# Gated delta rule of all chunks at once, its output made token by token inside the state chain

## What is computed

```
def gated_delta_rule(q, k, v, log_g, beta):          # 4 heads of 128, chunks of tokens
    gc = cumsum(log_g within the chunk)
    decay = exp(where(causal, gc_i - gc_j, -inf))
    kb = k * beta
    lower = where(strict, (kb @ k^T) * decay, 0)
    sol = triangular_solve(I + lower, [v * beta, kb * exp(gc)])
    u_base, w = sol
    attn = where(causal, (q @ k^T) * decay, 0)
    q_dec, k_dec = q * exp(gc), k * exp(g_last - gc)
    for each chunk, in order:
        u = u_base - w @ S
        o = q_dec @ S + attn @ u
        S = S * exp(g_last) + k_dec^T @ u
o_gdn = rms_norm(o, o_gain) * silu(gz)               # norm over the 128 of a head
mix   = concat([o_fox, o_gdn]) @ w_out
```

## Time and profile before

| quantity | value |
|---|---|
| median of 3 runs | 4125.67 us (4125.08 to 4134.72) |
| profiled execution, its time | 4139.84 us |
| profiled execution, its span | 4138.1 us |
| mean granted TensorE clock | 0.905 of full |
| busy: TensorE matmul, VectorE, ScalarE, GpSimd | 84%, 41%, 17%, 15% of the span |
| gated rule, third phase | 421.8 to 571.1 us |
| output stage, fourth phase | 571.1 to 588 us |
| forgetting attention, fifth phase | from 588.85 us |

### The profile page before, as it was taken

One profiled execution on the slowest core, in us unless ns is written; L12 is line 12 of the kernel. 1 busy time (PEld: TensorE's weight loads), 2 busy tenths in 40 slices (PEclk: granted clock), 3 DMA queues, 4 the chain that ended last, 5 costly groups with the idle time before them and its releaser, 6 DMA issues. The chain is left out here.

```text
span 4138.1 us, 48435 instructions
## 1 busy us (share of the span) xinstructions
PE 3482.5 (84%) x16676; PEld 2455.7 (59%) x16676; DVE 1704.2 (41%) x4271; ACT 697.8 (17%) x1515; POOL 605.8 (15%) x516
## 2 busy tenths in 40 slices
PE   8998768999989477998998688888779977788886
PEld 7875646887866476787786434333357764333433
DVE  2113333111122643211124576677512336676774
ACT  1001121101001111110122122222111311222221
POOL 0000000000000000000000244444300004444442
PEclk9998557999999788999998899999999998999999
DMA  4441002443422000343332599999842328999995
GB/s 169 147 151 71 0 0 76 145 156 122 151 108 99 2 3 2 122 154 132 136 130 100 237 421 421 421 422 422 357 156 83 131 92 355 421 422 421 422 421 207
DMA packets 113651, 828.17 MB, mean 200 GB/s; under 512 B 12528, under 2 KB 14064, under 8 KB 15120
## 3 DMA queue, kind: packets, MB, share of 16 engines
q0 software_dynamic: 73728, 536.90, 31.2%
q1 hardware_dynamic: 37184, 273.59, 18.0%
q10 hardware_dynamic: 2576, 15.59, 1.0%
HBM read 824.99 MB, written 1.05 MB: 200 GB/s over the span
## 5 line engine op out<-in xcount | busy, mean ns | idle before, releaser
L2090 PE MATMUL psum_all<-expert_rows,const_sb 128*128 128x512 f32 x2048 | 988.3, 641 | 265.0 <-ACT const_sb L2036 263.4
L1881 POOL DMA_INDIRECT expert_rows<-in_peer_uv_dram,head_experts x512 | 605.6, 1183 | 3463.5 <-issue 2434.3
L2090 PEld LDWEIGHTS psum_all<-expert_rows,const_sb 128*128 128x128 f32 x2048 | 409.9, 204 | 826.2 <-issue 488.4
L1971 DVE CUSTOM_DVE_ANT_0 expert_rows<-expert_rows,xn 128x1024 f32<-128x1024 f32 x512 | 618.5, 1224 | 312.2 <-DMA expert_rows<-in_peer_uv_dram,head_experts 307.1
L261 PE MATMUL psum_all<-xn,weight_ring 128*128 128x272 f32 (+1 forms) x3200 | 732.3, 392 | 0.0
L261 PEld LDWEIGHTS psum_all<-xn,weight_ring 128*128 128x128 f32 x3200 | 613.4, 192 | 118.8
L261 PE MATMUL psum_all<-hidden,weight_ring 128*128 128x272 f32 (+1 forms) x1408 | 318.6, 389 | 0.0
L261 PEld LDWEIGHTS psum_all<-hidden,weight_ring 128*128 128x128 f32 x1408 | 267.5, 190 | 50.5
L1599 PE MATMUL psum_all<-x,weight_ring 128*128 128x256 f32 x1024 | 229.0, 382 | 0.0
L2036 ACT ACTIVATE const_sb<-cst,head_weights 128x128 f32<-128x128 f32 x512 | 163.7, 390 | 321.4 <-DVE head_weights L1977 318.3
L1599 PEld LDWEIGHTS psum_all<-x,weight_ring 128*128 128x128 f32 x1024 | 192.9, 191 | 28.6 <-issue 2.9
(11 more groups left out here) (480 smaller groups left out, 3333.2 us busy)
## 6 DMA issues: line engine op xcount, KB each, us to landing
weight_ring<-in_ffn_in_dram SPq DMA_DIRECT2D x88, 1024.0 KB, 4.8
weight_ring<-in_w_in_dram SPq DMA_DIRECT2D x48, 1024.0 KB, 5.0
weight_ring<-in_ffn_out_dram SPq DMA_DIRECT2D x32, 1408.0 KB, 6.0
weight_ring<-in_peer_q_dram SPq DMA_DIRECT2D x16, 1024.0 KB, 7.9
weight_ring<-in_hyb_in_dram SPq DMA_DIRECT2D x12, 1024.0 KB, 4.8
wv<-in_w_v_dram ACTq DMA_DIRECT2D x8, 1024.0 KB, 7.7
weight_ring<-in_br_attn_dram SPq DMA_DIRECT2D x8, 1024.0 KB, 5.9
weight_ring<-in_br_lru_dram SPq DMA_DIRECT2D x8, 1024.0 KB, 6.5
```

The source lines that it names most:

```text
L1881: pool.indirect_dma_start(out=rows[:, j, :], out_offset=None, in_=a["peer_uv"], in_offset=bass.IndirectOffsetOnAxis(ap=idx[:, n, j:j + 1], ...
L1971: dve.tensor_tensor_reduce(row, row, xt[:, n, :], 1.0, 0.0, ALU.mult, ALU.add, dots[:, n, j:j + 1]).then_inc(S.dotted, 1)
L2090: mm = pe.matmul(sums(n, half), diag[:, j, :], rows[:, j, D + half * 512:D + (half + 1) * 512], start=False, stop=last and j == TOPK - 1)
```

## The change

The third phase handles all ten blocks at once: scores of the five chunks into three banks and the last blocks of each kind into others, turns by matmul against the identity in five groups, one solve with ten blocks, then a written-out chain over the chunks. `NL` of the solver takes its place in the idle region of the weight ring. A function `beside` lets VectorE make the attention products behind the solver's masks. The output of a chunk is made with tokens on partitions (`ot`), copied out by ScalarE, its squares summed by VectorE along the free axis, root on ScalarE, scaled, turned by TensorE, and multiplied by gain and gate into `mixed`, up to three steps behind the state. The fourth phase is removed. Silu of the gate goes to the end of ScalarE's stream in the first phase. The loops become straight code.

```diff
@@ solve_dve
         for l in range(1, LEVELS):
             last = level(l)
+        if beside is not None:
+            beside()
@@ first phase, ScalarE
-                        act.wait_ge(S.silu_ready, 12)
+                        act.wait_ge(S.bank_free, 4 + NZ)
+                        act.activation(z[:, 20:24, PADC:PADC + T], z[:, 20:24, PADC:PADC + T], ACT.Silu).then_inc(S.silu_ready, 1)
+                        act.wait_ge(S.silu_ready, 13)
@@ third phase, VectorE
-                            step(dve.memset(state[:, :, :], 0.0))
...
-                            with step.loop(NC - 1, 6) as c:
-                                chunk(c, True)
-                            chunk(NC - 1, False)
+                            dve.tensor_scalar(rneg[ROW_A:64, :], cum[ROW_A:64, :], -1.0, None, ALU.mult).then_inc(S.negated, 1)
+                            dve.wait_ge(S.decay_scores, 1)
+                            dve.tensor_scalar(dmat[:, MAIN_COLS], score_main(DECAY), 0.0, None, ALU.min).then_inc(S.decays, 1)
+                            dve.tensor_scalar(dmat[:, LAST_COLS], score_last(DECAY), 0.0, None, ALU.min).then_inc(S.decays, 1)
+                            dve.wait_ge(S.d_exp, 1)
+                            dve.wait_ge(S.scores, 1)
+                            dve.scalar_tensor_tensor(out=sb_.NT[:, MAIN_COLS], in0=score_main(KEYS), scalar=-1.0, in1=dmat[:, MAIN_COLS], op0=ALU.mult, op1=ALU.mult)
+                            step(dve.scalar_tensor_tensor(out=sb_.NT[:, LAST_COLS], in0=score_last(KEYS), scalar=-1.0, in1=dmat[:, LAST_COLS], op0=ALU.mult, op1=ALU.mult))
+                            def attention():
+                                step(dve.tensor_tensor(blocks3(dmat[:, :]), blocks3(dmat[:, :]), const("incl").unsqueeze(1).to_broadcast([P, BLOCKS, C]), ALU.mult))
+                                dve.wait_ge(S.scores, 2)
+                                dve.wait_ge(S.turned_in, len(turns))
+                                dve.tensor_tensor(at[:, MAIN_COLS], score_main(QUERIES), dmat[:, MAIN_COLS], ALU.mult).then_inc(S.attn_ready, 1)
+                                dve.tensor_tensor(at[:, LAST_COLS], score_last(QUERIES), dmat[:, LAST_COLS], ALU.mult).then_inc(S.attn_ready, 1)
+                            solve_dve(dve, S, step, 0, BLOCKS, sb_, solver_banks, attention)
...
+                            for c in range(NC + 3):
+                                if 1 <= c < NC:
+                                    dve.wait_ge(S.r_product, c)
+                                    dve.tensor_tensor(R[:, :, :], vt[:, 2 * c:2 * c + 2, :], psum[2][:, 0:2 * P].rearrange("p (g n) -> p g n", g=2),
+                                                      ALU.subtract).then_inc(S.r_ready, 1)
+                                if 2 <= c < NC + 2:
+                                    sum_out(c - 2)
+                                if c >= 3:
+                                    finish(c - 3)
+                                if c < NC - 1:
+                                    dve.wait_ge(S.s_product, c + 1)
...
+                                    last.then_inc(S.state_ready, 1)
+                                    dve.wait_ge(S.state_ready, c + 1)
+                                if 2 <= c < NC + 2:
+                                    scale_out(c - 2)
@@ third phase, ScalarE
+                            for c in range(NC + 2):
+                                if c < NC:
+                                    act.wait_ge(S.u_product, c + 1)
+                                    act.activation(U[:, c % 2, :, :], psum[3][:, 0:2 * P].rearrange("p (g n) -> p g n", g=2), ACT.Copy).then_inc(S.u_ready, 1)
+                                if 1 <= c <= NC:
+                                    take_out(c - 1)
+                                if c >= 2:
+                                    root(c - 2)
@@ third phase, TensorE
+                            for c in range(NC):
+                                for h, g_, q in heads:
+                                    sel = const("sel_g64", slice(ROW_A, 64), h * C, C)
+                                    o = score_block(DECAY, 2 * c + g_)[q, :]
+                                    pe.matmul(o, sel, cum[ROW_A:64, tokens(c)], start=True, stop=False)
+                                    mm = pe.matmul(o, rneg[ROW_A:64, tokens(c)], sel, start=False, stop=True)
+                            mm.then_inc(S.decay_scores, 1)
...
+                            products(KEYS, kb)
+                            for n, (_, src, first, count, bank) in enumerate(turns):
+                                if n == 3:
+                                    pe.wait_ge(S.decays, 2)
+                                if n == 4:
+                                    products(QUERIES, gq)
+                                for b in range(count):
+                                    for h in ((first + b) % 2 * 2, (first + b) % 2 * 2 + 1):
+                                        q = slice((h % 2) * C, (h % 2) * C + C)
+                                        mm = pe.matmul(bank[q, b * P:(b + 1) * P], src[:, h, tokens((first + b) // 2)], ident, start=True, stop=True)
+                                mm.then_inc(S.turned, 1)
+                            pe.wait_ge(S.turned_in, len(turns) - 1)
+                            solve_pe(pe, S, 0, BLOCKS, sb_, solver_banks)
...
+                            for c in range(NC):
+                                before = state[:, c % 2, :, :]
+                                if c:
+                                    pe.wait_ge(S.state_ready, c)
+                                    for h, g_, q in heads:
+                                        mm = pe.matmul(psum[2][q, g_ * P:(g_ + 1) * P], kbg[:, h, tokens(c)], before[:, h, :], start=True, stop=True)
+                                    mm.then_inc(S.r_product, 1)
+                                    if c >= 2:
+                                        pe.wait_ge(S.o_read, c - 1)
+                                    for h, g_, q in heads:
+                                        pe.matmul(out_block(c, g_, q), qd[:, h, tokens(c)], before[:, h, :], start=g_ == 0, stop=False)
+                                if c >= 3:
+                                    turn_out(c - 3)
...
+                                if c:
+                                    inside(c - 1)
+                                pe.wait_ge(S.u_ready, c + 1)
...
+                            inside(NC - 1)
+                            for c in range(NC - 3, NC):
+                                turn_out(c)
@@ fourth phase (silu, squares, head sums, root, reciprocal, spreading, gain, gate): removed
```

More of the change, by code:

```diff
@@ L674, in hybrid @@
-                    heads = [(h, h // 2, slice((h % 2) * C, (h % 2) * C + C)) for h in range(GDN_H)]
-                    with phase(nc, *SOLVE, "chunk_in", "scores", "decays", "d_exp", "turned", "turned_in", "r_product", "r_ready",
-                               "u_product", "u_ready", "o_product", "o_read", "s_product", "dve_held") as (block, S):
+                    BLOCKS = NC * GDN_H // 2
+                    MAIN = 8
+                    rneg = sb4("row_negative", [64, TP])
+                    dmat = sb4("dmat", [P, BLOCKS * C])
@@ new lines, in _ @@
+                            for c in range(NC + 3):
[9 more added lines that the diff above has]
+                                    dve.wait_ge(S.s_product, c + 1)
+                                    for h, g_, _ in heads:
+                                        carried = psum[(4, 5)[h % 2]][:, g_ * P:(g_ + 1) * P]
+                                        if c:
+                                            last = dve.scalar_tensor_tensor(out=state[:, (c + 1) % 2, h, :], in0=state[:, c % 2, h, :],
+                                                                            scalar=eg[:, h, (c + 1) * C - 1:(c + 1) * C], in1=carried, op0=ALU.mult, op1=ALU.add)
+                                        else:
+                                            last = dve.tensor_copy(state[:, 1, h, :], carried)
+                                    last.then_inc(S.state_ready, 1)
+                                    dve.wait_ge(S.state_ready, c + 1)
+                                if 2 <= c < NC + 2:
+                                    scale_out(c - 2)
@@ L771, in _ @@
                                 mm.then_inc(S.u_product, 1)
+                                if c:
+                                    inside(c - 1)
                                 pe.wait_ge(S.u_ready, c + 1)
-                                for h, g_, q in heads:
-                                    o = psum[(6, 1)[h % 2]][:, g_ * C:(g_ + 1) * C]
-                                    pe.matmul(o, state[:, h, :], qdc[:, h, :], start=True, stop=False)
-                                    mm = pe.matmul(o, U[q, g_, :], at[q, g_ * C:(g_ + 1) * C], start=False, stop=True)
@@ L817, in hybrid @@
+                                if c < NC - 1:
```

(6 more changed lines are left out.)

195 lines of the change are left out of this document (78 added, 117 removed).

## The result

| | before | after |
|---|---|---|
| median | 4130.19 us (4125.08 to 4142.48, 4 runs) | 3984.48 us (3977.47 to 3988.59, 4 runs) |
| ratio after to before | | 0.9641, 95% interval 0.9614 to 0.9669 |
| profiled execution, its time and span | 4139.84 us, 4138.1 us | 3988.59 us, 3986.8 us |
| mean granted clock of TensorE | 0.905 | 0.924 |
| code packets of the queue that ends in "instruction", whole program | 91 | 60 |

The change made the kernel 3.6% faster, where 2.2% was forecast (92.5 us). The stage itself comes first, in the order of its steps. The view is the timeline of the kernel after (start, us, engine, line, operation, count of merged records, and in the bracket the idle time before it with what ended it).

A forecast was written before the change was run, and what follows sets the result against it. The gated rule was taken as a chain, not a load, 165.8 us with its output stage. Setup 21.7, solve 19.6, chain 30 and supply 2 make 73.3, saving 92.5: 4033 us, range 4020 to 4060.

The forecast's parts named there:

- the time of the other 3,970 us is not touched: Whole program outside the gated rule and its output stage: claimed to keep its time, so all saving comes from the 165.8 us.
- instruction supply: New stage's straight code of some 520 TensorE matmuls: 2 us of waiting for instructions, bounds 0 and 3.5.
- decays, 80 records: Decay-score matmuls at the start of the stage's setup: 0.107 us a record, 8.6 us, bounds 4.3 to 12.3.
- rest of the setup: From the decays' end to the first Y product: masks, key and query products, turns, copies; 13.1 of 21.7 us.
- solve of ten blocks: One solver pass for ten blocks instead of five for two: 19.6 us, bounds 18.5 and 31.
- state chain: Chunk-after-chunk state updates and last output: 30 us, taken between 33.5 at slow and 25.9 at full clock.
- everything at full clock: Rival: setup, solve and chain all at full TensorE clock, stage 66 us, saved 100, 4026 us; chance 0.13.
- slow clock throughout: Rival: TensorE's granted clock stays at its lower level, stage 91 us, saved 75, 4051 us; chance 0.27.
- Not batched in effect: Rival: streams wait so ten blocks cost five passes, 58 us of solver stay, saved 52, 4074 us; chance 0.01.
- The slower case: Rival: instruction stalls in the solver's straight TensorE code, 9.5 us a packet for 0.3% slower, 4138 us and above; chance 0.02.
- VectorE's setup: Rival: masks and attention products run serially behind a late last turn, 3 to 4 us more, 4037; within the likeliest case's 0.57.
- the level: One level of the ten-block solve, six products of 20 records: 3.9 us at clock 1.00, 6.4 at 1.2 GHz.

## Why the prediction was wrong

The direction was right and the size was not: 3984.5 us lies below the range of 4020 to 4060.

**The step that failed** is the sentence that the time of the other 3,970 us is not touched. The instruction supply stood in the forecast as 2 us of cost inside the new stage, and as a rival with a price in stalls there. The evidence was in its own rows: 42 code packets and gaps ended by issue in RWKV. It was read as a price of code as such, when it was a loop whose code is fetched again every turn. Adding straight code ahead of that loop moved it to a place where it is held, which took 46.2 us from the loop, almost a third of the whole gain. The padded kernels show it from both sides: 64 instructions take 48.4 us out of the loop of before, 128 put 23 us back into that of after. A kernel whose loop had been held could have lost by the same move, and the forecast had no case for either. Of the 58.8 us by which the saving was missed, this step is 46 and the stage 12. Where the loop came to stand was not planned: this part of the gain is luck.

**The terms of the stage.** The sum was 73.3 us, measured 59.2 up to the last end:

| term | forecast | after | |
|---|---|---|---|
| decays, 80 records | 8.6 | 4.5 | 0.056 a record; near the lower bound, not 0.107 |
| rest of the setup | 13.1 | 11.5 | clock up at about 430.5, not 438 |
| solve of ten blocks | 19.6 | 19.2 | level 3.86, forecast 3.9 |
| state chain | 30 | 24.1 | clock stayed; bound 25.9 |
| instruction supply | 2 | 0 | |

The decays have 64 columns and were priced with the rate of 128, although the working had half of it as its lower bound, put the key products, also 64 columns, at 0.06, and gave the reason for that end: the shape no longer changes. The records of 0.154 us stand where 128 and 32 rows alternate; with one height 80 records ran at 0.056 while the clock was still 1.2 GHz. Two slips moved nothing: the rows give 0.10 and not 0.107 us at 128 columns, and VectorE's steps after 431.2 add up to 440.5 and not 441.5. The chain was placed between its two clocks by the drop between RWKV's solves. That analogy was wrong in part: the clock of the chain was 0.93. The drop that served as the model, 0.54 from 1423.58 on, comes behind the gap for want of code that ends at 1420.19 and does not speak of products and waits that alternate: with 64 instructions ahead of the loop, where that gap is gone, the same place reads

```profile
1423.80:1427.20 3.40, 3.28 (x109) 3.14 (x103) 2.72 (x6) 0.00 (x0) 0.00 (x0) 1.00 0.02 5
```

and from the first to the fifth turn the clock is 0.99 there, against 0.87. The Trainium skill's rule ("TensorE: Matmul & The Clock Gate", Part 1) that sustained busy time releases the full rate, which the prediction set aside for the rows at 0.50, would have given 26 us for the chain and was the better guide to this stage: TensorE was busy without a gap from 422.61 and had the rate from 430.5. It does not sort every case here: in the five small solves TensorE was busy for 82% of the time and at 1.2 GHz. The row that spoke against it, 3.41 us busy at 0.50, holds 12 records, where 3.50 us of the change at the same clock hold 56.

By these terms alone, everything at full clock (the rival at 4026) was the nearest case for the stage, though the decays still ran at 1.2 GHz: 104.9 us to the attention's first matmul, 4125.7 - 104.9 = 4021, still inside the range. It had 0.13.

**The rivals.** The slow clock throughout was wrong for the batch and right for the case that it should have been tied to: with five solves in place of one, TensorE fell to 1.2 GHz and stayed. "Not batched in effect" gave 58 us of solver; 57.5 were measured where it was made so. The slower case, 9.5 us of stall a packet in the stage, did not happen: the stage shows no gap for instructions on its matmuls. VectorE's setup was the bound at its very end: the product that X is copied from was done at 436.7, but the causal mask and the attention products kept VectorE until 437.6, and the first Y product waited 1.54 us for the copy. That is about 1 us and not 3 to 4.

**The steps that held.** The start at 422.6; the level; that sums and scalings fit into VectorE's waits; the table load for Sqrt in ScalarE's idle time (467.37, 1.28 us, behind the copies of U and of the output and ahead of the first root); silu and the DMA queues at no cost, as nothing ahead of the stage moved by more than 0.5 us.

## What to carry to other kernels

Where a profile shows waits ended by issue at the head of a loop and code packets that grow with its turns, the loop's code is being fetched again: count packets for each turn, and try some dozens of instructions ahead of it (64 gave 1% here, 192 half of that, 256 nothing) before anything else is done to the stage. Every edit ahead of such a loop can have a second effect of either sign, here about 1%, that has nothing to do with its purpose; compare the distances inside the unchanged loop before a gain is put down to the edit. On TensorE keep products of the same operand height together. A solve of ten blocks in one pass kept 2.4 GHz where five passes of two lost it.

## What was not expected of the hardware

- A loop of about 1,680 TensorE instructions costs 7 packets for five turns in some places; 64 instructions earlier or 128 later it costs 42 or 43 packets and 4 to 9 us a turn. The place within a packet of 256 decides, as the runs with 256 show; in one place between, four of five turns were fetched and one was not.
- A stand for want of instructions (2.89 and 2.40 us at the head of a turn) was followed by 1.2 GHz: over four turns the granted clock was 0.87 with the gaps of before and 0.98 and 0.99 without (after, and before with 64), and the same records were busy for 144.3, 125.8 and 124.9 us.
- Matmuls whose operand heights (128 and 32 rows) alternate take 0.154 us a record, and 0.056 (the decays of the change) when they don't, at the same clock.
- TensorE kept 2.4 GHz through the state chain though it was busy for only 15.3 of 24.6 us, while in the five small solves it was busy for 16.4 of 20 us (from 460 on) and stayed at 1.2 GHz. What separates the two was not settled.
